# Eight column sums of squares in the first mixer: one fp32 matmul each, or two fp32r passes over a rounded square and its remainder

## What is computed

```python
def l2norm(x, eps=NORM_EPS):
    return x * lax.rsqrt(jnp.sum(x * x, axis=-1, keepdims=True) + eps)

def gated_deltanet_mixer(q, k, v, z, b, a, conv_w, A_log, dt_bias, norm_w):
    qkv = jax.nn.silu(causal_depthwise_conv(jnp.concatenate([q, k, v], axis=-1), conv_w))
    q, k, v = jnp.split(qkv.astype(jnp.float32), 3, axis=-1)
    q, k, v = l2norm(heads(q)), l2norm(heads(k)), heads(v)
```

## Time and profile before

| | |
|---|---|
| median of 3 runs | 2350.09 us |
| lowest and highest of them | 2349.7 and 2351.44 us |
| the profiled execution, its own time | 2351.85 us |
| its span in the profile | 2350.1 us |
| TensorE busy in the span | 99% |
| VectorE, ScalarE, GpSimd busy | 55%, 39%, 6% |
| granted TensorE clock | full speed in all 40 slices |
| tiles 2 to 12 of `mix_in` and what stands between them | 395 to 465 us from the span's start |

### The profile page before, as it was taken

One profiled execution on the slowest core, in us unless ns is written; L12 is line 12 of the kernel. 1 busy time (PEld: TensorE's weight loads), 2 busy tenths in 40 slices (PEclk: granted clock), 3 DMA queues, 4 the chain that ended last, 5 costly groups with the idle time before them and its releaser, 6 DMA issues.

```text
span 2350.1 us, 32493 instructions
## 1 busy us (share of the span) xinstructions
PE 2315.3 (99%) x12487; PEld 1893.8 (81%) x12487; DVE 1303.0 (55%) x1988; ACT 919.8 (39%) x1447; POOL 140.6 (6%) x141
## 2 busy tenths in 40 slices
PE   8999999999999999999999999999999999999999
PEld 7888887788888888887977888888876668888887
DVE  4434336776544434357967766634336874766633
ACT  4222225634532223245444333424135873333323
POOL 3000001012000000030001000001010002000001
PEclk9999999999999999999999999999999999999999
DMA  5333323321233332332213333232753103333331
GB/s 152 95 98 98 99 90 81 81 72 56 70 93 98 98 98 90 99 100 63 64 55 108 90 98 98 90 98 90 174 160 94 44 28 97 90 98 98 99 99 72
DMA packets 319683, 215.86 MB, mean 92 GB/s; under 512 B 49321, under 2 KB 302796, under 8 KB 319576
## 3 DMA queue, kind: packets, MB, share of 16 engines
q1 hardware_dynamic: 316312, 200.43, 29.9%
q0 software_dynamic: 3264, 13.94, 1.8%
HBM read 212.20 MB, written 8.44 MB: 94 GB/s over the span
## 4 chain that ended last, share of the span: by engine, by line
PE 89%; DVE 5%; ACT 3%; DMA 1%; POOL 1%; issue 1%; POOLq 0%; SPq 0%; ACTq 0%; DVEq 0%
PE bank L649 18%; PE bank L651 17%; PE bank L650 17%; PE bank L837 7%; PE bank L839 7%; PE bank L838 6%; PE bank L1029 2%; PE bank L2976 1%; DMA raw<-in_nsa_w_in 1%; PE bank L3015 1%; PE bank L643 1%; DVE wL L487 1%; ACT arena L3202 1%; PE bank L644 1%; PE bank L645 1%
## 5 line engine op out<-in xcount | busy, mean ns | idle before, releaser
L649 PE MATMUL bank<-xH,wH 128*128 128x512 f32 x1904 | 751.7, 395 | 4.2 <-DVE wL L487 3.3
L651 PE MATMUL bank<-xH,wL 128*128 128x512 f32 x1904 | 741.5, 389 | 0.0
L650 PE MATMUL bank<-xL,wH 128*128 128x512 f32 x1904 | 741.0, 389 | 0.0
L487 DVE TENSOR_TENSOR wL<-raw,wH 128x1024 fp32r<-128x1024 f32 x355 | 440.8, 1242 | 497.1 <-ACT wH L444 496.6
L444 ACT ACTIVATE wH<-raw 128x1024 fp32r<-128x1024 f32 x355 | 374.1, 1054 | 711.1 <-PE bank L651 338.1
L649 PEld LDWEIGHTS bank<-xH,wH 128*128 128x128 f32 x1904 | 357.4, 188 | 87.7 <-issue 10.4
L650 PEld LDWEIGHTS bank<-xL,wH 128*128 128x128 f32 x1904 | 357.6, 188 | 76.3 <-issue 3.4
L651 PEld LDWEIGHTS bank<-xH,wL 128*128 128x128 f32 x1904 | 357.5, 188 | 74.9
L2672 ACT ACTIVATE arena<-arena,par 128x512 f32<-128x512 f32 x88 | 63.5, 724 | 271.9 <-DVE arena L2704 271.9
L837 PE MATMUL bank<-g_hi,wH 128*128 128x512 f32 x352 | 137.2, 390 | 0.7 <-DVE wL L487 0.7
L837 PE MATMUL bank<-xH,wH 128*128 128x512 f32 x352 | 137.0, 389 | 0.8 <-DVE wL L487 0.8
(11 more groups left out here) (385 smaller groups left out, 2894.0 us busy)
## 6 DMA issues: line engine op xcount, KB each, us to landing
raw<-in_ffn_w_in SPq DMA_DIRECT2D x88, 512.0 KB, 3.8
raw<-in_w_up SPq DMA_DIRECT2D x88, 512.0 KB, 3.8
raw<-in_ffn_w_out SPq DMA_DIRECT2D x44, 512.0 KB, 3.5
raw<-in_w_down SPq DMA_DIRECT2D x44, 512.0 KB, 3.5
raw<-in_w_mix_in SPq DMA_DIRECT2D x28, 512.0 KB, 3.9
raw<-in_w_kv_shared SPq DMA_DIRECT2D x12, 512.0 KB, 5.2
rel_wide<-rel_rows POOLq DMA_DIRECT2D x12, 512.0 KB, 11.4
arena<-rel_wide POOLq DMA_DIRECT2D x12, 448.0 KB, 4.4
```

What stands on the lines that cost most here:

```text
L487: nc.vector.tensor_tensor(lo[:, 0:n], raw[:, k, 0:n], hi[:, 0:n].bitcast(F32), ALU.subtract)\
L649: pe.matmul(o, wh, xa, start=a, stop=False)
L650: pe.matmul(o, wh, xb, start=False, stop=False)
L651: last = pe.matmul(o, wl, xa, start=False, stop=z)
```

## The change

ScalarE's square of units 0 to 7 now goes, rounded to fp32r, to `u_hi` (two halves of a tile whose room in the arena is free at that time). GpSimd makes the same square in float32 into `sq`, and then the remainder `sq - u_hi`, rounded to fp32r, into `u_lo`. TensorE multiplies a matrix of ones in fp32r (one column `one_r`, read 128 times over) by `u_hi` and then by `u_lo`, both added up in the same bank. The other sums of `sum_features` stay as they were. VectorE gets one small instruction, the rounding of the column of ones.

```diff
+        one_r = sb("one_r", [P, 1], F32R)
+        u_hi, u_lo = xH4[:, 4:6], xH4[:, 6:8]
+        u_hi_f = xH4f[:, 4:6]
...
+            nc.vector.tensor_copy(one_r[:], ones[:, 0:1])
...
             if t < 8:
                 act.wait_ge(sem("qkv_silu"), t + 1)
-                squares(act, t, U[:, 28 + t, :])
+                if t >= 2:
+                    act.wait_ge(sem("sum_mix"), t - 1)
+                nc.scalar.activation(u_hi[:, t % 2, :], U[:, 28 + t, :], ACT.Square).then_inc(sem("sq_mix"), 1)
...
         def gdn_pool(pool):
+            for t in range(8):
+                unit_low_pool(pool, t)
...
-                    pool.wait_ge(sem("lvl"), FOLDED + 1)
+                    pool.wait_ge(sem("lvl"), FOLDED + 17)
...
+        def unit_low_pool(pool, t):
+
+            pool.wait_ge(sem("qkv_silu"), t + 1)
+            nc.gpsimd.tensor_tensor(sq[:, t % 2, :], U[:, 28 + t, :], U[:, 28 + t, :], ALU.mult)\
+              .then_inc(sem("lvl"), 1)
+            pool.wait_ge(sem("lvl"), FOLDED + 2 * t + 1)
+            pool.wait_ge(sem("sq_mix"), t + 1)
+            nc.gpsimd.tensor_tensor(u_lo[:, t % 2, :], sq[:, t % 2, :], u_hi_f[:, t % 2, :], ALU.subtract)\
+              .then_inc(sem("lvl"), 1)
...
         def unit_sum_pe(pe, t):
+            if t == 0:
+                pe.wait_ge(sem("decay_dve"), 2)
             if t >= 4:
                 pe.wait_ge(sem("norm_mix"), t - 3)
-            sum_features(pe, t, bank[4 + t % 4], ones)
+            column_of_ones, o = one_r[:].broadcast_to([P, P]), bank[4 + t % 4][:]
+            pe.wait_ge(sem("sq_mix"), t + 1)
+            pe.matmul(o, column_of_ones, u_hi[:, t % 2, :], start=True, stop=False)
+            pe.wait_ge(sem("lvl"), FOLDED + 2 * t + 2)
+            pe.matmul(o, column_of_ones, u_lo[:, t % 2, :], start=False, stop=True).then_inc(sem("sum_mix"), 1)
```

## The result

The changed kernel's median is 2356.75 us over 11 runs (2354.47 to 2363.21). The kernel before, run 11 times beside it and before, has a median of 2352.59 us (2349.7 to 2359.36); the 2350.09 from which the prediction started was the median of its first three runs. The ratio is **1.0022, with a 95% interval of 1.0015 to 1.0030**: 3.5 to 7.1 us slower. The prediction said 2351.3, +1.2 us, within 2347.7 to 2354.0, and gave a chance of 0.06 to a change over 0.2% to the slow side. The direction was right, and so was most of where the time goes; the size was not, and the measured time is outside the range.

The account below looks back on a forecast made before the run. TensorE was taken as the bound, with VectorE as late or later at tiles 5 and 6. Terms -0.2 + 1.95 + 0.65 - 0.82 + 0.43 - 0.82 = +1.2 us gave a median of 2351.3 us, range 2347.7 to 2354.0.

Parts of the forecast that it names:

- 0.41 us saved for each sum: On TensorE, an fp32 sum costs 0.86 us and two fp32r passes 0.46; 3.3 us for eight sums.
- GpSimd and VectorE take turns: At SBUF reads: a GpSimd operation getting in between two dependent VectorE taps costs VectorE 0.93 us.
- VectorE bounds tiles 5 and 6: TensorE is the bound generally, but at tiles 5 and 6 VectorE is as late, or later.
- the loss stays to the end: Behind tile 11 VectorE and TensorE are late by the same, +1.2 us, and nothing is tied to a fixed time.
- one new wait for GpSimd at unit 5: At tile 9, TensorE waits 0.8 us for GpSimd's subtraction before unit 5's second pass.
- Unit 2 costs nothing: Unit 2's GpSimd pair comes after the last tap, covered by the 3.34 us reciprocal; otherwise tile 5 up to 1 later.
- up to 2.4 was forecast: Expected profile sign: GpSimd's two new operations take 1.28 us alone and up to 2.4 with a turn in them.
- Tile 6, the scans: Unit 3's square delays the first scan by 0.63; back-to-back scans shut the subtraction out; tile 6 starts 2.4 later.
- Tile 9: Unit 5's subtraction comes 0.06 after VectorE's remainder has begun, delaying the second pass: +0.43, +2.05 in all.
- Tile 5: Eviction +0.39, first tap delayed 0.43, subtraction between taps +0.93; tile 5 starts 1.75 us later.
- held for its whole length: Rival: whoever comes second waits the other's full length, 1.25 per turn; +3.2, 2353.3; chance 0.15 shared with subtraction between scans.
- The subtraction between the scans: Before tile 6, unit 3's subtraction gets in between VectorE's scans: +1.1 more, +2.3 total; chance 0.15 shared with whole-length holding.

Follow-up runs that it names:

- run 11: Not a follow-up run's label but part of "run 11 times": the unchanged kernel before, run 11 times beside the changed one, median 2352.59 us.
- the filling passes: Changed kernel plus twelve extra TensorE passes ahead of unit 2's sum, in the idle time before tile 6: stretch 68.63 us twice, changed kernel 69.97; ratio 1.0018.
- the idle time alone: Kernel before plus one more VectorE reciprocal of 4x512 behind the scans, so TensorE idles before tile 6: stretch 70.12 us against 65.31.
- the operations alone: Kernel before, with its fp32 sums, plus sixteen GpSimd operations writing to spare room, TensorE not waiting for them: stretch 69.49 us against 65.31; ratio 1.0018.
- the run with one pass: Changed kernel with one fp32r pass over the rounded square, no GpSimd operation and no remainder: stretch 63.20 us, median 2350.79; ratio to kernel before 0.9990.

## Why the prediction was wrong

Most of the mechanism was right: 0.41 us saved for each sum, GpSimd and VectorE take turns, VectorE bounds tiles 5 and 6, the loss stays to the end, and one new wait for GpSimd at unit 5. Two things were not: that the reciprocal is no matter to GpSimd, and that TensorE's idle time costs no more than its length. In the profiles the sum of +1.2 was 3.5 us too small (+4.66 in the stretch), in these terms:

- **"Unit 2 costs nothing"**, the step that failed. It rested on the assumption that an instruction with one input from SBUF does not matter to GpSimd. For evictions from PSUM that holds (the squares of units 1 and 2 both ran beside one), for the reciprocal it does not. The prediction said itself that it might cost up to 1. It cost +1.1, not at tile 5 as that clause had it, but at tile 6 by way of the next taps (3.40 us for three instead of 2.30). Shown by the run without unit 2's pair (tile 6 earlier by 1.05). The reciprocal's own row stayed at 3.34, as was said; it is GpSimd's row of 4.93, where up to 2.4 was forecast, that gives it away.
- **Tile 6, the scans: +1.1.** The first scan cost +0.73 (forecast +0.63). The subtraction did get in before the second, +1.03, which had been the alternative at +1.1: it was asked for at 421.03, 0.13 before the second scan. That VectorE's back-to-back instructions shut GpSimd out was read from one row, beside instructions of 128x512 and 128x1024. Why it got in between two scans of 0.4 us is not shown. What it cost is shown by the run without both pairs.
- **The clock, +1.35**, was in no term and no rival. An idle time of 3 us was not foreseen because the first two terms were too small; but a wait that a change adds should be priced with it. Shown by the filling passes and by the idle time alone.
- Tile 9: +0.8 instead of +0.43, which is +0.4, by a race between two requests that was called with 0.06 us and fell the other way.
- Tile 5 went 0.5 better than said, which hid a part of the rest by luck. Unit 0's first operation cost 0.66 and not 0.93, so the eviction of tile 3 was 0.12 late and not 0.39. Unit 1's taps lost 1.10 and not 1.36, since the held square needed only 0.90 more.

1.1 + 1.1 + 1.35 + 0.4 - 0.5 = 3.45, which is the 4.66 less the 1.2. No rival had this sum: "held for its whole length" gave +3.2 by another cause (the turns cost 0.92, as in rows 6, and not 1.25), and GpSimd's operations are no longer than 1.24 to 1.30 alone. "The subtraction between the scans" did come true, and it is one term of five.

The range should have reached further, since two of its terms had only been bounded one at a time, and since the three runs of the kernel before, from which it started, lay 2.5 us below its median of eleven. That base alone nearly used up the 2.7 us between the forecast and the top of the range: from the median of eleven, +1.2 would have been 2353.8.

## What to carry to other kernels

GpSimd as a helper is not free when it reads SBUF. Here an operation of 1.3 us cost VectorE 0.7 to 1.0 us each time it got in between two of VectorE's two-input instructions, and one that was held back cost whichever instruction came next. So put such work only where the engine that it disturbs has spare time up to the next deadline, and take it out where that engine is the bound: three units of eight gave all of their saving, the other five gave a loss. Where a saving lies on an engine that waits anyway (tiles 5 and 6), it is worth nothing, and TensorE, made to wait 3 us, ran at half its clock afterwards.

## What the runs showed of the hardware

- VectorE's reciprocal of 4x512 (3.34 us, one SBUF input) kept a GpSimd operation that reads SBUF waiting: 4.93 us for an operation of 1.28, in all five profiles that have the pair of unit 2 there (the change, the operations alone and the filling passes); memsets in the same place took 1.28 and 1.27.
- A GpSimd operation that reads SBUF and was held until VectorE had made a remainder ended 0.90 us behind that remainder, twice in the change, although it takes 1.28 alone.
- A tensor-scalar operation on VectorE of 0.47 us took 1.65 beside a GpSimd memset, and was not delayed beside GpSimd's reading square.
- TensorE's granted clock fell to 0.50 to 0.51 for five to eight passes in five profiles with an idle time of 1.9 to 3.1 us: the change (twice) and the idle time alone, in tile 6, and the operations alone and unit 2 left out, in tile 5. The slow passes did not always come right behind the idle time: with the operations alone they began 1.3 us into tile 5, with unit 2 left out 1.0 us into it, and with the idle time alone 0.8 us into tile 6. After 2.5 us at tile 5 the clock did not fall in the change itself (twice), in the two runs with filling passes and in the one without the pairs of units 2 and 3, nor after 2.0 us in the run with one pass. What decides this stays open.
